# Spreading gate rows over features in a hybrid mixer: f32 rows over 6 partitions, and rounded rows with their rest over 38

## What is computed

```python
proj = h @ w_in                                   # 512 x 3342
beta = sigmoid(b)                                 # 6 heads, one number per token and head
g = -exp(a_log) * softplus(a + dt_bias)
G = cumsum(g, axis=-1)                            # within chunks of 64 tokens
rhs = concat([v * beta[..., None], kb * exp(G)[..., None]])   # kb = k * beta
q_dec = q * exp(G)[..., None]
k_dec = k * exp(G[..., -1:] - G)[..., None]
```

## Time and profile before

| | |
|---|---|
| median of 3 runs | 2798.63 us (2798.47 to 2802.38) |
| profiled execution | 2792.82 us |
| its span, first to last instruction | 2790.7 us |
| TensorE busy | 2647.9 us, 95% |
| VectorE busy | 1576.8 us, 57% |
| ScalarE busy | 1187.8 us, 43% |
| GpSimd busy | 310.5 us, 11% |
| mean granted TensorE clock | 0.977 |

### The profile page before, as it was taken

One profiled execution on the slowest core, in us unless ns is written; L12 is line 12 of the kernel. 1 busy time (PEld: TensorE's weight loads), 2 busy tenths in 40 slices (PEclk: granted clock), 3 DMA queues, 4 the chain that ended last, 5 costly groups with the idle time before them and its releaser, 6 DMA issues. The chain is left out here.

```text
span 2790.7 us, 55442 instructions
## 1 busy us (share of the span) xinstructions
PE 2647.9 (95%) x23093; PEld 2121.3 (76%) x23093; DVE 1576.8 (57%) x1951; ACT 1187.8 (43%) x1525; POOL 310.5 (11%) x356
## 2 busy tenths in 40 slices
PE   8999899999999988999999998998789999999998
PEld 7677678888777757788888887844778787788887
DVE  6747454344474655667776666467445555454462
ACT  5544342132454443555665554353215343432232
POOL 5022000000110401011111111021310000000002
PEclk9999999999999999999999999999979999999999
DMA  4200234334220022887777875311014252334241
GB/s 136 79 9 3 61 104 115 83 90 109 80 79 20 4 54 96 285 283 278 279 279 283 288 280 181 88 38 57 4 33 129 76 145 65 100 90 113 80 115 53
DMA packets 351895, 331.31 MB, mean 119 GB/s; under 512 B 17273, under 2 KB 269525, under 8 KB 351605
## 3 DMA queue, kind: packets, MB, share of 16 engines
q1 hardware_dynamic: 348101, 317.76, 36.4%
q0 software_dynamic: 3392, 11.14, 1.1%
q10 hardware_dynamic: 240, 0.07, 0.0%
HBM read 317.41 MB, written 11.53 MB: 118 GB/s over the span
## 5 line engine op out<-in xcount | busy, mean ns | idle before, releaser
L3128 DVE TENSOR_TENSOR experts_w_lo<-experts_raw,experts_w_hi 128x2048 fp32r<-128x2048 f32 (+1 forms) x81 | 167.8, 2079 | 79.8 <-ACT experts_w_hi L3084 78.6
L3128 DVE TENSOR_TENSOR experts_w_lo<-raw_in_act,experts_w_hi 128x2048 fp32r<-128x2048 f32 (+1 forms) x81 | 166.9, 2077 | 58.3 <-ACT experts_w_hi L3084 58.0
L3084 ACT ACTIVATE experts_w_hi<-raw_in_act 128x2048 fp32r<-128x2048 f32 (+1 forms) x81 | 139.7, 1746 | 49.0 <-DMA raw_in_act<-in_moe_up 43.5
L3297 PE MATMUL experts_psum<-experts_w_hi,experts_xg_lo 128*128 128x512 f32 x384 | 154.6, 402 | 5.2 <-DVE experts_w_lo L3128 4.1
L1574 PE MATMUL proj_psum<-keep_act_hi,proj_w_lo 128*128 128x512 f32 x360 | 151.6, 421 | 5.9 <-DVE proj_w_lo L1494 5.9
L3299 PE MATMUL experts_psum<-experts_w_hi,experts_xg_hi 128*128 128x512 f32 x384 | 150.4, 392 | 0.0
L3298 PE MATMUL experts_psum<-experts_w_lo,experts_xg_hi 128*128 128x512 f32 x384 | 150.3, 391 | 0.0
L3084 ACT ACTIVATE experts_w_hi<-experts_raw 128x2048 fp32r<-128x2048 f32 (+1 forms) x81 | 140.3, 1741 | 21.7 <-DMA experts_raw<-in_moe_gate 14.8
L1576 PE MATMUL proj_psum<-keep_act_hi,proj_w_hi 128*128 128x512 f32 x360 | 141.3, 393 | 0.0
L1575 PE MATMUL proj_psum<-keep_act_lo,proj_w_hi 128*128 128x512 f32 x360 | 141.0, 392 | 0.0
L831 PE MATMUL conv_ffn_psum<-keep_act_hi,conv_ffn_w_lo 128*128 128x512 f32 x336 | 132.0, 393 | 2.0 <-DVE conv_ffn_hid_lo L880 2.0
(11 more groups left out here) (896 smaller groups left out, 6833.9 us busy)
## 6 DMA issues: line engine op xcount, KB each, us to landing
raw_in_act<-in_moe_gate SPq DMA_DIRECT2D x33, 1024.0 KB, 7.1
experts_raw<-in_moe_up SPq DMA_DIRECT2D x32, 1024.0 KB, 10.3
experts_raw<-in_moe_down SPq DMA_DIRECT2D x32, 768.0 KB, 11.7
raw_in_act<-in_moe_down SPq DMA_DIRECT2D x32, 768.0 KB, 6.9
conv_ffn_raw<-in_w_ffn_in SPq DMA_DIRECT2D x43, 512.0 KB, 5.0
experts_raw<-in_moe_gate SPq DMA_DIRECT2D x17, 1024.0 KB, 8.9
raw_in_act<-in_moe_up SPq DMA_DIRECT2D x16, 1024.0 KB, 5.2
proj_raw<-in_w_in SPq DMA_DIRECT2D x18, 768.0 KB, 4.3
```

The lines of the kernel that those rows point to most:

```text
L3084: act.activation(w_hi[v % 2][:, s], raw[ring][:, 0:n], ACT.Copy).then_inc(rounded, 1)
L3128: dve.tensor_tensor(w_lo[v % 2][:, s], raw[ring_of(2 * v + q)][:, 0:n], w_hi[v % 2][:, s].bitcast(F32), ALU.subtract).then_inc(split, 1)
L3297: pe.matmul(out, lhs[1][:, first + k, :], w_hi[slot][:, cols], start=begin and k == 0, stop=False)
```

## The change

The three row slots are no longer read by TensorE in f32. A new tile `spread_of` takes the place of the three slots in `mix_fab`, in the fp32r kind. Partitions 0 to 5 hold a row rounded by ScalarE, partitions 32 to 37 its rest by VectorE, and the partitions between are zero. `head_rows` becomes fp32r too and holds its six rows twice, at 0 and at 32. One product over 38 partitions then gives rounded part plus rest. The f32 rows are made in two new tiles `row0` and `row1`; `row0` is used twice, and so the second exponential waits for the first rest.

```diff
 def make_early_masks(m, pool, rows, done):
...
+    pool.tensor_copy(m.head_rows[:, :], rows[:, :]).then_inc(done, 1)
+    pool.wait_ge(done, 6)
+    pool.tensor_copy(m.head_rows[LOW_ROWS, :], rows[0:6, :]).then_inc(done, 1)
...
+        pool.memset(spread_of[0:HD, :, :].bitcast(F32), 0.0).then_inc(zeroed, 1)
...
+    def round_row(act, q, src, made_by, done):
+        act.wait_ge(done, made_by)
+        act.activation(spread_of[R, q, :], src[R, :], ACT.Copy).then_inc(row_high, 1)
+
+    def rest_of_row(dve, n, q, src):
+        dve.wait_ge(row_high, n)
+        dve.tensor_tensor(spread_of[LOW_ROWS, q, :], src[R, :], spread_of[R, q, :].bitcast(F32), ALU.subtract).then_inc(row_low, 1)
...
         if h == 4:
             act.wait_ge(g_dve, 4)
-            act.activation(small[R, 1, :], g[R, :], ACT.Exp).then_inc(g_act, 1)
+            act.activation(row[0][R, :], g[R, :], ACT.Exp).then_inc(g_act, 1)
+            round_row(act, 1, row[0], 6, g_act)
...
         if h == 6:
-            act.wait_ge(g_dve, 7)
-            act.activation(late[R, :], t2[R, :], ACT.Exp).then_inc(g_act, 1)
+            round_row(act, 0, row[1], 7, g_dve)
+            act.wait_ge(row_low, 1)
+            act.activation(row[0][R, :], t2[R, :], ACT.Exp).then_inc(g_act, 1)
+            round_row(act, 2, row[0], 7, g_act)
...
     def start(dve, group):
+        if group == 0:
+            dve.wait_ge(zeroed, 1)
...
-            gate_step(dve, 7, dve.reciprocal(small[R, 0, :], late[R, :]))
+            gate_step(dve, 7, dve.reciprocal(row[1][R, :], late[R, :]))
+            rest_of_row(dve, 1, 1, row[0])
             conv_of(dve, 1, (1,))
...
         if h == 7:
+            rest_of_row(dve, 2, 0, row[1])
+            rest_of_row(dve, 3, 2, row[0])
             conv_of(dve, 2, (1,))
...
     def spread_out(pe, p, q, bank):
-        pe.matmul(ps[:, bank, :], m.head_rows[0:6, p * P:(p + 1) * P], small[0:6, q, :], start=True, stop=True).then_inc(spread, 1)
+        pe.matmul(ps[:, bank, :], m.head_rows[0:38, p * P:(p + 1) * P], spread_of[0:38, q, :], start=True,
+                  stop=True).then_inc(spread, 1)
...
         if (h, f) == (11, 0):
-            pe.wait_ge(g_act, 7)
+            pe.wait_ge(row_low, 3)
...
+        fab_at = -(-m.nc.sbuf_base // 32) * 32
         fab = mix.sb("fab", [P, 4, T])
+        spread_of = m.nc.alloc_sbuf_tensor_at(m.name("spread_of"), [P, 3, T], F32R, offset=fab_at + T * 4)
```

More of the change, by code:

```diff
@@ L132, in setup_phase @@
     nc = m.nc
-    rows = row_params(m)
-    total = sum(len(names) * n for names, _, n, _, _ in rows)
+    params = row_params(m)
+    total = sum(len(names) * n for names, _, n, _, _ in params)
     stages = -(-total // P)
@@ L150, in setup_phase @@
         stage = ph.sb("stage", [P, stages, P])
-        xs = ph.sb("xs", [P, TT, D])
+        xs, rows = ph.sb("xs", [P, TT, D]), ph.sb("rows", [P, 3 * P])
         ps = ph.banks()
@@ L157, in setup_phase @@
         places, at = [], 0
-        for names, src, n, width, twice in rows:
+        for names, src, n, width, twice in params:
             for v, name in enumerate(names):
@@ L181, in _ @@
                                pattern=[[-1, P]], channel_multiplier=1).then_inc(const, 1)
-            make_early_masks(m, pool, masked)
+            make_early_masks(m, pool, rows, masked)
         @block.sync
@@ L907, in ffn_phase @@
     dense_phase(m, jobs, "ffn", norm_of(m, "norm2_0"), then)
+LOW_ROWS = slice(32, 38)
 def mask_buffers(m, persist):
@@ L918, in mask_buffers, with make_early_masks @@
     m.reset = persist.sb("reset", [P, T])
-    m.head_rows = persist.sb("head_rows", [P, 3 * P])
+    m.head_rows = persist.sb("head_rows", [P, 3 * P], F32R)
     m.causal = persist.sb("causal", [P, P])
-def make_early_masks(m, pool, done):
+def make_early_masks(m, pool, rows, done):
     pool.memset(m.reset[:, :], 1.0).then_inc(done, 1)
-    pool.memset(m.head_rows[:, :], 1.0).then_inc(done, 1)
+    pool.memset(rows[:, :], 1.0).then_inc(done, 1)
     pool.wait_ge(done, 2)
@@ L929, in make_early_masks @@
     for base, step, mult in ((0, 1, -HD), (HD - 1, -1, HD)):
-        pool.affine_select(out=m.head_rows[:, :], in_=m.head_rows[:, :], compare_op=ALU.is_ge, fill=0.0, base=base,
+        pool.affine_select(out=rows[:, :], in_=rows[:, :], compare_op=ALU.is_ge, fill=0.0, base=base,
                            pattern=[[step, 3 * P]], channel_multiplier=mult).then_inc(done, 1)
         pool.wait_ge(done, 4 if base == 0 else 5)
+    pool.tensor_copy(m.head_rows[:, :], rows[:, :]).then_inc(done, 1)
+    pool.wait_ge(done, 6)
+    pool.tensor_copy(m.head_rows[LOW_ROWS, :], rows[0:6, :]).then_inc(done, 1)
 def make_masks(m, pool, done):
@@ L1595, in dn_aside @@
     F = slice(HD, HD + 6)
-    small, late = fab[:, 1:4], fab[:, 3]
+    late = fab[:, 3]
+    row = [ph.sb(f"row{q}", [P, T]) for q in range(2)]
+    spread_of = mix["spread_of"]
     ea = ph.sb("ea", [P, 1])
@@ L1607, in dn_aside @@
     f_act, f_dve, gated = (ph.sem(n) for n in ("f_act", "f_dve", "gated"))
+    zeroed, row_high, row_low = (ph.sem(n) for n in ("zeroed", "row_high", "row_low"))
     masks_done = ph.sem("masks_done") if l == 0 else None
@@ L2575, in groups @@
                                                               (1932, fxp[:, 3:6]), (1152, dn[:, 9:12]), (2316, fxp[:, 6:9]))]
-            mix_tiles = dict(dn=dn, fxp=fxp, xp=xp, fab=fab)
+            mix_tiles = dict(dn=dn, fxp=fxp, xp=xp, fab=fab, spread_of=spread_of)
             woven_phase(m, "proj", groups, norm_of(m, f"norm1_{l}", full=cv[:, 0:8]),
```

## The result

The changed kernel takes 2882.24 us (median of 5 runs, 2872.64 to 2886.66) against 2802.28 for the kernel before (5 runs, 2798.47 to 2802.99): a ratio of 1.029, 95% interval 1.028 to 1.031. It is 80 us slower where the prediction said 10 us faster. Its profiled execution took 2882.66, with a span of 2880.4. Two runs on record were disturbed, 11630.57 us of e5 (its median without it is 2792.12) and 2965.49 of the kernel before beside it, and are left out of the ratios.

The account below looks back on a forecast made before the run. TensorE, busy for 95% of the span, was taken as the bound. Terms -11.3 + 0.7 + 0.3 = -10.3 took the profiled 2792.8 to 2782.5 us, and the median, 5.8 above, to 2788.3; range 2783 to 2793.

Parts of the forecast that it names:

- The product's price: Projection phases, TensorE: each of 18 spreading products falls from 0.86 to 0.23 us, gaining 11.3 us.
- The group's price: Projection phases, TensorE: 0.39 us paid once per group of spreading products, tied to few rows; forecast to stay.
- The rival that goes by the Trainium skill: Few rows cost nothing extra in the rounded kind, so the 0.39 goes too: -15.0 us, 2783.6; chance 0.12.
- VectorE, 0.7 at half 8: Layer 0 projection: the first added subtraction delays the next weights' rest, TensorE's wait growing from 0.75 to about 1.45 us.
- layer 1 would be covered: Layer 1 projection: TensorE arrives later after a clock fall, and the 0.85 us between covers the subtraction's 0.7.
- The dip's 1.6 us: Layer 1, half 7: without the clock fall, 0.7 is paid but 1.6 us (7 products) comes back.
- Half 7's subtractions, free: Projection, VectorE: the other two subtractions, 1.4 us, fall into a 0.79 wait and idle time, costing nothing.
- ScalarE, 0.3 in layer 1: End of layer 1's projection: logarithms moved by 0.7 free the head sum's bank late, charged 0.3 us.
- The sum over the two phases, -10.3: Both layers' projection phases: -11.3 for the products, +0.7 for VectorE, +0.3 for ScalarE.
- 18 spreading records instead of 36: Sign to look for in the changed kernel's trace: each spreading product leaves one TensorE record instead of two.
- Its order is untouched: Projection phase: TensorE's order stays the same, given as a reason that its new wait does no harm; no size.
- The rival that ended slower: Longer waits or moved gaps set off falls of the granted clock, 1.6 us each, from ten on: 2804.3; chance 0.04.

Follow-up runs that it names:

- e5: Changed kernel with 54 empty TensorE instructions ahead of the experts' loop; 2792.53 us, ratio 0.9985 to the kernel before.
- e12: Changed kernel with 36 empty TensorE instructions ahead of the experts' loop and the six lone spreading products over 128 zero-padded rows; 2782.11 us, ratio 0.9942.
- e1: Changed kernel with 36 empty TensorE instructions ahead of the experts' loop; 2785.69 us, ratio 0.9944 to the kernel before.
- e6: Changed kernel with 72 empty TensorE instructions ahead of the experts' loop; 2787.90 us, ratio 0.9963 to the kernel before.
- e8: Changed kernel with 18 empty TensorE instructions ahead of the experts' loop; 2790.06 us, ratio 0.9971 to the kernel before.
- e13: Changed kernel with 36 empty TensorE instructions in the setup phase, 18 at each of two idle places; 2789.68 us, ratio 0.9967.

## Why the prediction was wrong

Its steps, one by one:

- **The product's price.** 18 records instead of 36, 1.31 and 1.08 where 1.3 and 1.1 were forecast. Right: the kind of the operands sets 0.23 or 0.86, also over 38 rows.
- **The group's price stays.** Right, and for the reason given, few rows (e12). The rival that goes by the Trainium skill, TensorE: Matmul & The Clock Gate, section Why this matters for your kernels, by which few rows cost nothing extra, falls: 0.39 us a group disagree.
- **VectorE, 0.7 at half 8.** Right. In e1, VectorE and then TensorE:

```profile
85.15 0.68 DVE L1699 TENSOR_TENSOR spread_of<-proj_row,spread_of 6x512 fp32r<-6x512 f32 x1
85.86 2.07 DVE L1791 SCALAR_TENSOR_TENSOR dn_cv<-mix_dn,keep_params,dn_cv 128x511 f32<-128x511 f32 x3
87.85 1.75 DVE L1500 TENSOR_TENSOR proj_w_lo<-proj_raw,proj_w_hi 128x1536 fp32r<-128x1536 f32 x1
```

```profile
89.75 0.47 PE L1580 MATMUL proj_psum<-keep_act_hi,proj_w_lo 128*128 128x512 f32 x1 [1.46 <-DVE proj_w_lo L1500]
```

  The wait of the earlier trace rows went from 0.75 to 1.46; 1.45 was forecast. That layer 1 would be covered held only where the clock fell ahead of it: in the changed kernel half 7 runs at a clock of 1.00 and the wait is there as well, 1.49 at 794.20. The dip's 1.6 us did not come back for it, as the prediction had it for that case: from the start of half 7 to that of half 8 it is 9.95 (784.25 to 794.20), as long as with the dip before (789.96 to about 799.9), since VectorE sets it.
- **Half 7's subtractions, free.** Right: 1.28 together at 96.94 in e1, and the convolution behind them no longer waits its 0.79.
- **ScalarE, 0.3 in layer 1.** Right. TensorE at the head sum, before, then after:

```profile
815.05 0.40 PE L1576 MATMUL proj_psum<-keep_act_hi,proj_w_hi 128*128 128x512 f32 x1
815.28 1.02 PE L1915 MATMUL proj_psum<-dn_a_flat,keep_pair_ones 128*128 128x512 f32 x2
```

```profile
809.44 0.39 PE L1582 MATMUL proj_psum<-keep_act_hi,proj_w_hi 128*128 128x512 f32 x1
809.99 1.10 PE L1942 MATMUL proj_psum<-dn_a_flat,keep_pair_ones 128*128 128x512 f32 x2 [0.16 <-ACT dn_a_flat L1739]
```

  From start to start it was 0.23 and is 0.55, 0.32 late, and in e1 0.52.
- **The sum over the two phases, -10.3.** Measured -10.1, of it -5.0 (forecast -4.95) and -5.1 (-5.35).
- **The step that failed** is the one between that sum and the kernel's time: "the profiled execution ... would take 2782.5" lets everything outside the phases keep its length. "18 spreading records instead of 36" stood in the text as a sign to look for, and "Its order is untouched" as a reason for calm. That these records are also instructions, and that everything behind them moves up by 36, was in no step. At the good places the changed kernel takes 2785.7 to 2792.5 (e1, e5, e6, e8, e13), all within the range of 2783 to 2793, though with medians that scatter by 7 us this confirms the range and not the term of 10.3; the phases do that. At its own place 94 us are added in the loop, 13.5 at each of seven jumps. The rival that ended slower had 0.04 and the wrong mechanism, falls of the clock by waits in the projection phase; the clock did fall, but behind the experts' fetch stops.

## What to carry to other kernels

A shorter program is a moved program. Where an engine runs a long loop, here of 1678 of TensorE's instructions, compare the instruction queue's packets on the page before and after any edit ahead of it: a count that grows by several for each jump back (here 123 to 186) points to a refetch. Some empty instructions in an idle place took it away here; leaving out a few warm-up products brought it, so either can move a loop. Judge a small edit by the length of the phase that it touches as well as by the kernel's time, which clock falls elsewhere move by more than the edit. And a lone product over a few rows among full ones was cheaper here when padded with zeros to 128; for the pairs that was not tried.

## What the runs showed of the hardware

- Stops for instructions can carry a data name: five of the seven first stops, 26.1 us, are put down to "DVE experts_w_lo"; at the second pass that step had been done 5.3 us before. They also carry a clock price: after two stops of some 5 us, some ten products ran at the 1.2 GHz level, and the phase's mean clock was 0.92 instead of 0.99.
- A jump back to a loop that is refetched stops TensorE for 4.4 to 5.9 us, by the place once or twice a pass. During the two stops shown the DMA engines are full with data, 0.98 and 1.00 of their time, 320 and 384 GB/s; whether a stop would be shorter without that was not tried.
- Empty TensorE instructions with a semaphore update take 0.145 us each over 256 of them (37.2 us), 0.153 each from 72 to 256.
- Leaving the full array for a product over 38 rows and coming back costs 0.39 to 0.40 us a group in the rounded kind too, as over 6 rows in plain f32.
